# The first mixer of a two-block model as one woven block instead of seven stages

## The reference

```python
def _ab_streams(h, w_in, gate_b):
    q_m, k_m, v_m, o_m, g_m, q_a, k_a, v_a = _split(h @ w_in, AB_WIDTHS)   # 512 x4, 16, 512, 128, 128
    g = g_m.reshape(b, s, 2, 2, H_M) + gate_b
    ...
def _mixer_ab(hl, hc, w_in, gate_b, norm_w, sink, w_out, ctx_out):
    ml, gl, ol, (ql, kl, vl) = _ab_streams(hl, ...)       # latent
    mc, gc, oc, (qc, kc, vc) = _ab_streams(hc, ...)       # context
    outs = [_directional(_mlstm_scan, mc + gc[d], ml + gl[d], init, d == 1) for d in range(2)]
    cos, sin = _axial_rope(hl.shape[1])
    a_lat = _window_attention(_rope(ql, cos, sin), _rope(kl, cos, sin), vl, kc, vc, sink)
    y_lat = _merge_ab(outs[0][1] + outs[1][1], ol, a_lat, norm_w, w_out)
    ...
    y_ctx = _merge_ab(outs[0][0] + outs[1][0], oc, _context_attention(qc, kc, vc, sink), norm_w, w_out)

def _merge_ab(m, o, a, norm_w, w_out):
    hm = _head_norm(m, norm_w) * jax.nn.sigmoid(o)
    return jnp.concatenate([hm, a], -1) @ w_out
```

## Time and profile before

| | |
|---|---|
| median of three runs | 4579.09 us |
| the profiled execution | 4576.1 us, its span 4574.0 us |
| busy: PE, DVE, ACT | 4068.3 us (89%), 3106.2 us (68%), 1815.2 us (40%) |
| HBM | 164 GB/s over the span |
| mean granted TensorE clock | 0.93 |

### The profile page before, as it was taken

One profiled execution on the slowest core, in us unless ns is written; L12 is line 12 of the kernel. 1 busy time (PEld: TensorE's weight loads), 2 busy tenths in 40 slices (PEclk: granted clock), 3 DMA queues, 4 the chain that ended last, 5 costly groups with the idle time before them and its releaser, 6 DMA issues. The chain is left out here.

```text
span 4574.0 us, 66054 instructions
## 1 busy us (share of the span) xinstructions
PE 4068.3 (89%) x25626; PEld 3599.1 (79%) x25626; DVE 3106.2 (68%) x6951; ACT 1815.2 (40%) x2848; POOL 7.6 (0%) x14
## 2 busy tenths in 40 slices
PE   6957789999998999999979769999999786988888
PEld 5635689998886999988868459999788676977687
DVE  2154669677886686778972468877788666755775
ACT  2122344443333344443432234444333543544354
POOL 0000000000000000000000000000000000000000
PEclk9975799999999999999989889999999898988899
DMA  4211147555665685557652026655666321442143
GB/s 186 107 60 75 59 142 231 172 172 192 244 239 210 259 315 163 169 203 254 244 187 85 34 88 210 208 171 166 233 247 243 128 96 46 189 146 86 44 167 134
DMA packets 122582, 755.23 MB, mean 165 GB/s; under 512 B 15629, under 2 KB 17165, under 8 KB 58146
## 3 DMA queue, kind: packets, MB, share of 16 engines
q1 hardware_dynamic: 122274, 751.02, 46.0%
HBM read 695.39 MB, written 55.57 MB: 164 GB/s over the span
## 5 line engine op out<-in xcount | busy, mean ns | idle before, releaser
L1362 DVE TENSOR_TENSOR expert_ring_low<-expert_ring,expert_high 128x1024 fp32r<-128x1024 f32 x768 | 935.3, 1219 | 267.0 <-ACT expert_high L1575 266.5
L1575 ACT ACTIVATE expert_high<-expert_ring 128x1024 fp32r<-128x1024 f32 x768 | 811.3, 1057 | 651.9 <-PE ps L1526 651.0
L1494 PE MATMUL ps<-peer_hT_high_peer,expert_high 128*128 128x256 f32 x3072 | 887.1, 289 | 10.0 <-DVE expert_ring_low L1362 9.8
L1496 PE MATMUL ps<-peer_hT_high_peer,expert_ring_low 128*128 128x256 f32 x3072 | 865.6, 282 | 0.0
L1495 PE MATMUL ps<-peer_hT_low,expert_high 128*128 128x256 f32 x3072 | 865.5, 282 | 0.0
L1494 PEld LDWEIGHTS ps<-peer_hT_high_peer,expert_high 128*128 128x128 f32 x3072 | 588.5, 192 | 12.7 <-DVE expert_ring_low L1362 11.8
L1495 PEld LDWEIGHTS ps<-peer_hT_low,expert_high 128*128 128x128 f32 x3072 | 589.0, 192 | 0.0
L1496 PEld LDWEIGHTS ps<-peer_hT_high_peer,expert_ring_low 128*128 128x128 f32 x3072 | 583.7, 190 | 0.0
L1526 PE MATMUL ps<-expert_high,weighted_high 128*128 128x512 f32 x1536 | 476.5, 392 | 24.4 <-DVE weighted_low L1389 24.4
L1526 PE MATMUL ps<-expert_ring_low,weighted_high 128*128 128x512 f32 x1536 | 475.1, 391 | 0.0
L1526 PE MATMUL ps<-expert_high,weighted_low 128*128 128x512 f32 x1536 | 474.8, 390 | 0.0
(11 more groups left out here) (592 smaller groups left out, 6940.9 us busy)
## 6 DMA issues: line engine op xcount, KB each, us to landing
expert_ring<-in_peer_u SPq DMA_DIRECT2D x192, 1024.0 KB, 5.3
expert_ring<-in_peer_v SPq DMA_DIRECT2D x192, 1024.0 KB, 4.8
gelu_peer<-gelu_out SPq DMA_DIRECT2D x192, 256.0 KB, 5.5
gelu_in_peer<-gelu_peer SPq DMA_DIRECT2D x96, 512.0 KB, 5.7
weight_ring<-in_ffn_w_up SPq DMA_DIRECT2D x22, 2048.0 KB, 7.3
weight_ring<-in_w_in SPq DMA_DIRECT2D x14, 2048.0 KB, 7.3
weight_ring<-in_w_mod SPq DMA_DIRECT2D x12, 2048.0 KB, 9.5
weight_ring<-in_peer_wq SPq DMA_DIRECT2D x12, 2048.0 KB, 7.4
```

Source lines behind the costliest of these rows:

```text
L1362: dve.tensor_tensor(piece(low, n), piece(raw, n), high[:, n % LEAD, :].bitcast(F32), ALU.subtract).then_inc(low_done, 1)
L1494: pe.matmul(o, b[:, s], hT_h[:, c, :], start=(c == 0), stop=False)
L1496: mm = pe.matmul(o, lo[:, s], hT_h[:, c, :], start=False, stop=(c == DC - 1))
L1575: act.activation(high[:, n % LEAD, :], piece(raw, n), ACT.Identity).then_inc(high_done, 1)
```

## The change

`project`, `mlstm_gates`, `mlstm`, `head_norm`, `rope`, the mask load and `attend` of this mixer become one block of seven kinds of generators, merged by planned times. The turned input keeps its own stage. Weight columns are packed anew: unit 0 holds keys (128 columns), values (128) and all gates in one set of 100 rows with gaps, and comes first; then output gate, qa, and q, k, v of the recurrence. A job is over a piece of at most 256 weight columns, with two PSUM banks in alternation for all. Keys are projected once, and PE makes the copy per head and its rotated form with constant matrices; values are projected turned and turned back by PE. The gates of both directions stand on partitions 0 to 3 and 32 to 35 and are scanned together. Modulation units 4 to 11 all run beside the recurrence. Squares of the head norm go to ACT. The mLSTM mask is stored in 5 blocks of 256 columns, the row selector is replaced by a broadcast column of the identity, and the q.k products of a head pass through one bank, the weighted sums through one set of banks.

```diff
+pieces = [(0, 0, 256), (0, 256, 128)] + [(u, off, PIECE) for u in range(1, 6) for off in (0, PIECE)]
+start = [6, 17, 23, 34.5, 46, 57] + [68.5 + 20.6 * k for k in range(6)]
+period = [5.5] * 2 + [5.6] * 4 + [10.2] * 6
+jobs = [cols(0, 0, "s", B.kraw), cols(0, 1, "v", B.vaT), cols(1, 0, "s", B.g[0:64 + HALF, :], m=64 + HALF)]
+for h in range(2):
+    jobs += [rows(2 + h, t, "s", B.so[:, t, h * PIECE:(h + 1) * PIECE], func=ACT.Sigmoid) for t in range(4)]
+for n, (dst, scale) in enumerate(((B.qa, 1.0), (B.qT, 1.0), (B.kT, DH_M ** -0.5))):
+    for h in range(4):
+        jobs.append(cols(4 + 2 * n + h // 2, h % 2, "vs"[h % 2], dst[:, h, :], scale, dst_late=n == 2))
...
+    gates = Gates(G, S, B, in1, step, gate_job, 23)
+    rope = Rope(G, S, B, in1, step, kv_jobs, q_jobs)
+    attention = Attend(G, S, B, step, items, 75, (4.5, 2.3))
+    scan = Mlstm(G, S, B, in1, step, qk_jobs, attention, 190, 6.4)
+    norm = HeadNorm(G, S, B, in1, step, o_jobs, scan)
+    mods = ModAfter(G, S, B, in1, "mod_b", 4, attention, 193.5, 6.4)
...
+@block.tensor
+def _(pe):
+    gates, rope, attention, scan, norm, mods = parts(None)
+    weave(in1.tensor(pe), gates.tensor(pe), rope.tensor(pe), attention.tensor(pe), scan.tensor(pe), mods.tensor(pe))
...
+@block.scalar
+def _(act):
+    weave(in1.split_high(act), in1.out_s(act), gates.scalar(act), attention.scalar(act), scan.scalar(act),
+          norm.scalar(act), mods.scalar(act))
...
+@block.sync
+def _(sp):
+    for dst, src in consts:                      # 8 loads
+        sp.dma_start(dst, src).then_inc(S.consts_landed, 16)
+    ws.run_ahead(sp, u0 + 6)
+    sp.wait_ge(S.roped, 6)
+    sp.wait_ge(S.cols_out, 1)
+    sp.wait_ge(S.weighed, 4)
+    sp.dma_start(B.mask[:, :, :, :], G.d["scan_mask"]).then_inc(S.mask_landed, 16)
+    ws.run_ahead(sp)
```

The projection, whose groups of six products are the grain in which other PE work comes between:

```diff
+class In1:
+    def tensor(self, pe):
+        for k, j in enumerate(self.jobs):
+            parts = self.parts(j.piece)
+            for c in range(DC):
+                if c % 2 == 0:
+                    yield self.at[k] + self.span[k] * c / DC
+                if c == 0 and k >= 2:
+                    pe.wait_ge(*self.evicted(k - 2))
+                if j.piece != seen and c % 4 == 0:
+                    pe.wait_ge(self.S.low_done, 2 * j.piece + c // 4 + 1)
+                for x, y in PASSES:
+                    mm = pe.matmul(self.tile(k), ...)
...
```

The planned times of the recurrence, of its products and of the modulation, on PE and on ACT (t(n) = start + 2 + 6.4 n for combo n):

```diff
+class Mlstm:
+    def product_at(self, h, n):
+        return (self.start - 1 if h == 0 else self.t(2 * h - 1) + 0.2) + 1.2 * n
+    def products(self, pe, h):
...
+            if k >= 1:
+                pe.wait_ge(S.qk_out, k)
...
+    def weighted(self, pe):
...
+                yield self.t(n) + 6.5 + 0.7 * t
+                if t == 0:
+                    pe.wait_ge(S.w_ready, 4 * (n + 1))
+                    if n >= 1:
+                        pe.wait_ge(S.h_out, n)
...
+    def rows(self, pe):
...
+            yield self.t(n) - 2
...
+    def vector(self, dve):                       # distances, weights at t(n) + i; finish(n - 1) at t(n) + 4.9
...
+    def exps(self, act):                         # exp i at t(n) + 0.5 + i, after d_ready
...
+    def products_out(self, act, h):              # product_at(h, n) + 0.6, after qk_ready
...
+class ModAfter:
+    def tensor(self, pe):
+        for u in range(MODS):
+            yield self.start + self.period * u   # 16 records into 4 groups of 32 rows
...
+            if u >= 1:
+                yield self.start + self.period * u + 1
+                sums(u - 1)
+    def scalar(self, act):
+        for u in range(MODS):
+            yield self.start + self.period * u + 0.6
+            act.wait_ge(S.parts_ready, u + 1)
+            act.activation(B.part[:, u % 2, :], G.ps[:, u % 2, :], ACT.Identity).then_inc(S.parts_out, 1)
...
```

The attention has the same steps with two buffers for each (scores, probabilities, turned, values); items with 256 keys take maximum and exp from PSUM with no scaled copy. Its PE steps stand at 0, 4.6 and 7.2 us from an item's planned start, ACT's at 3.2 and 6.0, DVE's at 1.5, 5.4 and 8.6. The head norm:

```diff
+class HeadNorm:
+    def scalar(self, act):
+        for h in range(H_M):
+            for t in range(4):
+                yield self.done(h) + 0.3 * t      # done(h) = t(2 h + 2) + 5.5
+                act.wait_ge(S.h_out, 2 * h + 2)
+                act.activation(B.sq[:, t, :], ..., ACT.Square, accum_out=...)
+            if h >= 2:
+                yield self.done(h) + 2
+                act.activation(..., ACT.Sqrt).then_inc(S.rms_ready, 1)
...
```

More of the change, by code:

```diff
@@ new lines, in merged, with weave @@
+def merged(*programs):
+    due = [(next(p), n, p) for n, p in enumerate(programs)]
+    while due:
+        due.sort(key=lambda d: d[:2])
+        t, n, p = due.pop(0)
+        yield t
+        t = next(p, None)
+        if t is not None:
+            due.append((t, n, p))
+def weave(*programs):
+    for _ in merged(*programs):
+        pass
+class Buffers:
+    pass
+AB_ORDER = (5, 3, 4, 0, 1, 2)
+PIECE = 256
+HALF = 36
+D_AT = 32
+MODS = 8
+M1_SIGNALS = (
+    "v_ready s_ready v_out s_out high_done low_done "
+    "consts_landed mask_landed zeroed ones_set dve_step "
+    "dup_ready swapped roped va_turned va_out weighed "
+    "f_ready abs_ready log1p_ready exp_step m_ready em_ready nat_ready cols_ready cols_out "
+    "as_ready masked negmax_ready probs_ready sum_ready turned pT_ready pv_ready den_step rden_ready att_out "
+    "qk_ready qk_out mb_ready d_ready exp_ready w_ready num_ready num_step h_out "
+    "parts_ready parts_out mod_ready ms_ready rms_ready")
@@ new lines, in mixer_ab @@
+            B.v1 = sbuf(nc, "v1", [P, 4, H_M, 129], F32)
+            room = 2 * H_M * TOK * 4
+            gates = Arena(nc, nc.sbuf_base - room - 4 * H_M * 4, room)
+            B.xi, B.xf, B.t1, B.t2, B.one, B.zero = [gates.take(f"gate_{k}", [HALF, TOK], F32) for k in
+                                                     ("i", "f", "t1", "t2", "one", "zero")]
+            B.nat = gates.take("gate_nat", [HALF, 2, TOK], F32)
+            B.mask = sbuf(nc, "scan_mask", [P, 2, 5, SEQ], F32)
+            front = Arena(nc, nc.sbuf_base - 10 * SEQ * 4, 10 * SEQ * 4)
@@ new lines, in mixer_ab @@
+            B.sm = sbuf(nc, "scores", [P, 2, TOK], F32)
+            B.pr = sbuf(nc, "probs", [P, 2, TOK], F32)
+            B.pT = sbuf(nc, "probsT", [P, 2, TOK], F32)
+            B.kraw = B.pr[:, 0, :]
+            B.vaT = B.pT[:, 0, :]
+            B.wrow = B.pr[:, 1, :]
+            B.wm = sbuf(nc, "window_mask", [P, 2, TOK], F32)
+            late = Arena(nc, first, nc.sbuf_base - first)
+            B.qk = late.take("qk", [P, 2, QK_WIDTH], F32)
+            B.w = late.take("mlstm_w", [P, 2, QK_WIDTH], F32)
@@ L3751, in constants @@
     c["rope_swap"] = sw
+    copies = [a[:, g * DH_A + np.arange(P) % DH_A] for a in (c["ident"], sw) for g in range(H_KV)]
+    c["key_copies"] = np.stack(copies, 1)
     c["gla_masks"] = np.stack([chunk_masks(dr, 1 / GATE_TAU) for dr in range(2)], 1)
```

1055 lines of the change are left out of this document (611 added, 444 removed).

## The result

The changed kernel takes 4444.3 us (median of 4; 4440.2 to 4448.0) against 4576.8 us (4573.5 to 4579.5), a ratio of 0.9711 with the interval 0.9694 to 0.9727: 132.5 us less. Forecast were 134 us less and a time of 4445 us. Its profiled execution has a span of 4443.2 us at a mean granted clock of 0.944, before 0.930.

What follows compares the result with a forecast made beforehand. TensorE was taken to bound projection and attention, chains between DVE, ACT and PE the rest. Part A to 131, Part B 133 to 264, Part C 95 to 359 instead of 492.7: 134 us less, 4445 us, range 4410 to 4495.

Steps and rivals of the forecast that it cites:

- Part A: Block's start up to the first score, priced by PE's work: 74.6 us after a 2.4 us start, ending at 131.
- The stall for ACT's table changes: Before the first score: late evictions by ACT stall PE, 4 us taken between bounds 0 and 7.7.
- The slow clock at the start: At the block's beginning, before the first score: 1.5 us added for PE's slow clock.
- 61.3 + 7.8: PE's work before the first score: 61.3 us projection jobs, 7.8 us added key copies, gate move, swaps and transposes.
- Part B: Attention woven with the last 16 projection jobs: 126.8 us on PE at full clock, 133 in all, to 264.
- the 6 us for split pieces: Attention woven with projection: split pieces fall into items' chains, 1 us in each of six, bounds 0 and 20.
- Part C: Recurrence with eight modulation units, paced by ACT's in-order queue: combos 8.8 and 12.1 us, 95 in all, to 359.
- Tight: Rival: the ACT order doesn't bite and PE bounds the recurrence; block ends at 333, 4419 us; chance 0.14.
- As loose as the second mixer: Rival: the block's PE work runs at 0.78 of full rate; block ends at 402, 4488 us; chance 0.26.
- Attention holds the clock down: Rival: attention woven with projection runs wholly at the lower clock level, another 127 us; 4572 us; chance 0.04.
- Slower: Rival: idle and short products hold 1.2 GHz in attention and recurrence; block ends at 545, 4631 us; chance 0.04.
- no overlap: Rival: one mis-ordered wait serialises the parts, attention begins after projection; time within 0.2% of now; chance 0.02.

Runs made afterwards that it cites:

- e6: Changed kernel with two more jobs of the gates' size (24 products of 512 columns each) in the projection ahead of the first score: 4452.9 us, ratio 0.9729.
- e5: Changed kernel with the last sixteen projection jobs back to back ahead of the attention, which then stands alone on PE: 4515.7 us, ratio 0.9865.
- e3: Changed kernel reordered: two products a combo, weighted sums in one run, products' copies and the modulation's part behind the exps: 4427.5 us, ratio 0.9674.
- e4: Changed kernel with the eight modulation units in a stage of their own behind the block, none beside the recurrence: 4458.0 us, ratio 0.9738.
- e1: Changed kernel with the modulation units 3 us later in the written order (196.5 instead of 193.5): 4427.3 us, ratio 0.9672.
- e2: Changed kernel with the next head's four q.k products made two in each of the two combos before it: 4450.2 us, ratio 0.9718.
- e7: e3 with the square root of the first three heads' norm, and their weighting, moved behind the last exp: 4417.5 us, ratio 0.9650.
- e9: The kernel of e7 once more, word for word: 4417.3 us, ratio 0.9649.

## Why the prediction was right, step by step

**Part A (first score at 131; measured 131.75).** The start held: first product at 56.5, 2.5 us in, where 2.4 stood. From there it took 75.2 us against 74.6, but two terms of that sum were wrong and cancelled. The stall for ACT's table changes, put at 4 us, was nothing. Seven changes came between 79 and 101 us, for one (timeline of ACT):

```profile
90.69 1.28 ACT L914 ACT_TABLE_LOAD   x1
91.98 0.63 ACT L914 ACTIVATE gate_t<-gate_t 36x512 f32<-36x512 f32 x1
92.64 1.28 ACT L802 ACT_TABLE_LOAD   x1
93.93 0.38 ACT L802 ACTIVATE sig_o<-ps 128x256 f32<-128x256 f32 x1
```

The window of that stretch:

```profile
90.00:95.00 5.00, 4.94 (x41) 4.74 (x41) 2.28 (x3) 4.90 (x8) 0.00 (x0) 1.00 0.00 0
```

ACT is busy 4.90 of 5 us, and PE 4.94: two PSUM banks were cover enough. The Trainium skill ("ScalarE: Activation LUTs", What ACT_TABLE_LOAD costs) has a load at about 1283 ns, which these rows show, and a drain of about 1380 ns with each switch, which they don't: the load starts 0.03 us behind the exp and the next eviction 0.01 us behind the load. The slow clock at the start, put at 1.5 us, was larger:

```profile
54.00:60.00 6.00, 3.48 (x8) 2.81 (x9) 2.96 (x3) 2.52 (x3) 2.79 (x5) 0.50 0.60 154
60.00:65.00 5.00, 5.00 (x19) 4.00 (x19) 0.00 (x0) 0.22 (x1) 0.00 (x0) 0.81 0.23 92
```

PE worked 3.5 us of the first window at the lower level and some 1.9 of the second (0.81 is 38% at half), which loses half of 5.4, 2.7 us. That leaves 3.4 us above my 61.3 + 7.8; it stands among the small products of keys, swaps and gates, and I haven't measured which. That PE bounds this part is shown by e6.

**Part B (133 us, to 264).** Clock 1.00, PE busy 132.3 of 133. The last projection product stands at 260.9 and the last value products at 257.5, so B took 129.3 us, and 1.7 of them went to the recurrence's first products and row, which stand between the last projection jobs (from 257.40 and 258.69). That leaves 127.6: the sum of rows, 126.8, was good, and the 6 us for split pieces were under 1. The price at full clock taken from the second mixer was the step that mattered. It held in the woven block, and e5 shows the other price.

**Part C (95 us; combos 8.8 and 12.1).** Measured 8.6 without products and 13.9 and 12.9 with them; with the root 12.8, where 8.8 + 2.6 = 11.4 stood (2.8 us of it are the slow sums at 332.42 and the slow unit behind them; in e3 and e4 this combo takes 10.5). Laid beside the forecast's marks: the first finish ends at 279.6 instead of 286.1 (3 us of these 6.5 come from B), the seventh 65.5 us later instead of 62.0, the last another 7.6 later instead of 5.0, and the tail takes 4.2 instead of 5.5. So the combos and the last sums cost 6 us more than I had, and the start and the tail 7.8 less; the end at 357 for 359 is in part a cancellation. That the time came within 1 us of the forecast is luck: single terms were off by up to 6.

The chain behind it was told right as to the modulation: e1 moves it and gets 17 us, e4 takes it away and finds DVE's 6.24. Of the next head's products and copies I had made too much: 3.3 us a combo, where they cost 1.8 when left in place beside late units (e1).

One thing the working left out is that PE's clock falls in part C. Behind a wait of 1.81 us eight weighted sums of the changed kernel take 2.06 us, where e4 has 1.05 (at 285.92) at the upper level:

```profile
288.34 2.06 PE L1131 MATMUL ps<-v,mlstm_w 128*128 128x129 f32 x8 [1.81 <-DVE cat L1172]
```

The next eight take 1.93, and the two pairs of product records between them 1.06 each instead of 0.60. Together that is some 2.8 us in this combo, more than the 1.8 that its 13.9 is above the forecast's 12.1. By these rows the chain at full clock is shorter than I had it, and the clock filled the gap: luck again. In e2 the clock made a combo of 11.2 out of 8.6. A wait alone doesn't decide it: e4 has three of 2.27 us, and only behind one of them do the sums slow down (1.93 for eight at 300.66; 2.92 for 24, the upper level, at 315.26).

**The rivals.** Tight (4419, block end 333): not by this order; e7 and e9, with another, reach its numbers, at 4417 and with the next stage at 334. As loose as the second mixer (4488): no, PE busy 279.4 of 305 us at clock 0.95, 1.00 and 0.86. Attention holds the clock down (4572): not woven; alone it stays at the lower level (e5). Slower (4631) and no overlap: no; 0.86 was the lowest clock of the three stretches.

**What is open.** Which operations keep the attention at the lower level when it stands alone; where the 3.4 us of part A are; what makes the clock fall in a PE that waits for nothing (e7, e9); and how e1's 17 us divide between the queues' order and the clock.

## What to carry to other kernels

Price a woven block engine by engine at full clock, then write down each in-order queue and ask of every instruction that another engine feeds: what stands behind it, and who waits for that? Here the modulation's small stream, in each combo a unit of 1.9 us on PE and a copy of 0.6 us on ACT, cost 17 us in eight combos by standing 3 us too early in the written order. The clock that fell behind the waits has a share in that, so look at the clock of every stretch before blaming a queue. In this kernel weaving dense products into a chain of short ones was worth more than the idle time that it filled: the same attention took 126 us at the upper level together with nearly all of some 67 us of projection, and 130 us at the lower level by itself.

## What was not expected of the hardware

- Attention alone, entered at PEclk 1.00, was at 0.50 within 7 us and stayed there for 123 us, though PE was busy 92% of them (e5). The fall itself came behind 3.3 us without work for PE.
- The clock fell for a moment while PE was busy 5.00 of 5.00 us and waited for nothing (e7, window below), at other places in the next execution. Each time cost 1.6 us. The DMA share of that window, 0.86, isn't the difference: it was 0.86 in 291:296 of the same execution as well, at clock 1.00.

```profile
281.00:286.00 5.00, 5.00 (x25) 4.28 (x24) 3.91 (x8) 2.91 (x10) 0.00 (x0) 0.66 0.86 367
```

- After a wait of 4.5 us the last 24 weighted sums took 5.37 us in e3, and 2.92 in e7 behind a wait of 0.80.
